# One group of the second block's modulation, moved from the heads' stage into an earlier norm

## The chip, the cores and the metric

The kernel runs on one core of one Trainium2 chip. The metric is the time of an execution on the device in microseconds (us); several executions were timed and their median counts.

## What is computed

Two transformer blocks in a row, 512 tokens of width 1024, all in float32. The first block: a mixer (RWKV and differential attention), a mixture of experts, and a token embedding that is gated and added. The second block has two layers, each with a mixer and a mixture of experts. Its norms and branches are modulated by vectors that depend on a condition `c` alone, not on the tokens:

```python
# first block, the end
ple_gate = jax.nn.sigmoid(rms_norm(x, norm_ple[l]) @ w_ple_gate[l])
x = x + ple_gate * (p[l] @ w_ple_proj[l])
# second block, for each layer l
mod = jax.nn.silu(c) @ ada_w[l] + ada_b[l]
mod_c = jax.nn.silu(c_ctx) @ ada_w[l] + ada_b[l]
sh1, sc1, g1, sh2, sc2, g2 = jnp.split(mod[:, None, :], N_MOD, axis=-1)
csh1, csc1, cg1, csh2, csc2, cg2 = jnp.split(mod_c, N_MOD, axis=-1)
h = modulate(rmsnorm(x, norm_mix_g[l]), sh1, sc1)     # h * (1 + scale) + shift
```

`ada_w` is 2 x 1024 x 6144. So the modulation is two rows times a matrix of 24 MB for each layer: almost all of it is the reading of the matrix.

## The kernel before

The program is a row of phases. Each is a block with its own semaphores, and a barrier of all engines closes it: the next phase starts when the latest engine of this one is done. A wait for that barrier shows in the trace as released by line 139. A scope that ends adds its semaphores to a list; when the list holds over 95 they are cleared, with one more barrier (line 144).

The modulation (`Modulation`, `ModulationSide`, line 2365 on) is cut into 2 x 3 groups `(l, g)`: layer `l`, 2048 of the 6144 columns. A group is carried as side work by some phase, and its result goes to the tensor `modD` in HBM, from which later norms load their scales and shifts as rows. The groups stand as follows: (0, 0) in `h1`, the heads' stage of the first block; (0, 1) in the differential attention `a1`; (0, 2) in the norm `ne` of the second block's first mixer; (1, 0) and (1, 1) in its heads' stage `he`; (1, 2) in the norm `no` of its second mixer. The groups of layer 1 are first read by `no`.

For one group the carrying phase does this:

- SyncE (`begin`, `sync`): 4 small loads of the bias, then 8 loads of 1 MB (128 partitions x 2048 columns, line 2420) into a ring of 3 buffers. From the fourth on a load is issued only when the matmuls of the piece three before it are done. At the end, 4 stores to `modD` (line 2413), and a wait for them.
- TensorE (`tensor`, lines 2451 and 2455): for each piece 4 matmuls with a moving operand of 512 columns and a stationary operand of 2 columns (each appears as two in the trace), and after the eighth piece 4 with the bias. The pieces are dealt out evenly over the phase's steps: with `total` pieces, step `s` of `steps` gets those from `total * s // steps` up to `total * (s + 1) // steps`.
- ScalarE (`scalar`, line 2435): 4 copies of 2 x 512 from PSUM, after all its other work in the phase.

`norm_phase` (line 201): ScalarE sums the squares of all tiles, a small chain gives the inverse root, VectorE scales tile by tile (line 303; with modulation also line 307), TensorE turns each tile with 8 transposes (line 324), ScalarE and VectorE write the high and the low half of the result (lines 179 and 184). The side work stands on TensorE behind the transposes of each tile. On SyncE it stands behind the loads of the gain and of `ahead`. `np` has 4 tiles, `ne` and `no` 6.

`ple` (line 2746) runs `np`, then `pq` (transposes of the embedding), then `lg` (the two matmuls, with their weights read in pieces of 256 KB). Its `early` loads the embedding, waits for it, and loads three pieces for `lg`, all on SyncE's queue during `np`.

`heads_phase` (line 504) in `he`: 12 jobs, in this order: four tiles of queries, four of keys (half as wide), then two of context queries and two of context keys. For each job VectorE scales and turns by the rotary tables (lines 597 to 610), TensorE transposes, ScalarE and VectorE split (lines 630 and 184). A second piece of side work, the pooling branch `PoolSide` (lines 2529, 2539, 2555, 2559, 2567), lies between. TensorE's order in a step is:

```python
for j, (i, t) in enumerate(jobs):
    if mix:
        mix.tensor(pe, j)
    if extra:
        extra.tensor(pe, j, len(jobs))
    pe.wait_ge(y_done, j + 1)
```

so that the transpose of job `j` stands behind the pieces of step `j`. After `he` comes the attention `ae`.

Of the kernel before, what the change touches and what calls it, by code (L numbers as in the profile page):

```python
# [194 lines left out]
def bc_row(ap, n):  # L195

    return ap.rearrange("(a n) -> a n", a=1).to_broadcast([P, n])
# [257 lines left out]
def linear(lhs, nk, tiles, W, cols, evac, on="v", behind=None):  # L455

    return dict(lhs=lhs, nk=nk, tiles=tiles, W=W, cols=cols, evac=evac, on=on, behind=behind)


def transpose_phase(nc, name, src, nt, nk, dst, tab, ahead=None):  # L460

    G = min(nk, 4)
    groups = [(t, k) for t in range(nt) for k in range(0, nk, G)]
    with Scope(nc, name) as s:
        banks = [s.ps(f"pt{i}") for i in range(4)]
        t_done, hi_done, lo_done = s.sem("t"), s.sem("hi"), s.sem("lo")
        block = s.block()

        def parts(i):
            t, k = groups[i]  # L470
            hi, lo = (d[:, k:k + G, t * P:(t + 1) * P] for d in dst)
            return hi, lo, banks[i % 4][:, 0:G * P].rearrange("p (k t) -> p k t", k=G)

        if ahead:
            @block.sync
            def _(sp):
                ahead.fetch(sp)

        @block.tensor
        def _(pe):  # L480
            for i, (t, k) in enumerate(groups):
                if i >= 4:
                    pe.wait_ge(lo_done, i - 3)
                for j in range(G):
                    mm = pe.transpose(banks[i % 4][:, j * P:(j + 1) * P], src(t, k + j), tab[:, C_IDENT:C_IDENT + P])
                mm.then_inc(t_done, 1)

        @block.scalar
        def _(act):
            for i in range(len(groups)):  # L490
                hi, _, bank = parts(i)
                act.wait_ge(t_done, i + 1)
                split_hi(act, hi, bank).then_inc(hi_done, 1)

        @block.vector
        def _(v):
            for i in range(len(groups)):
                hi, lo, bank = parts(i)
                v.wait_ge(hi_done, i + 1)
                split_lo(v, lo, bank, hi).then_inc(lo_done, 1)  # L500
# [2149 lines left out]
def operand(pair):  # L2650

    return lambda k, t: [h[:, k, t * P:(t + 1) * P] for h in pair]
# [90 lines left out]
            linear_phase(nc, "l5", [linear(operand(hT), KD, allt, A["w_out"], D, add_evac(xs))], ahead=ahead)  # L2743


def ple(nc, tab, A, xs):
    allt = lambda c: range(NT)
    with Scope(nc, "pl") as m:
        hT = m.pair("hT", [P, KD, SEQ])
        g = m.sb("g", [P, NT, D])  # L2750
        pt = m.sb("p", [P, NT, 256])
        pT = m.pair("pT", [P, 2, SEQ])
        p_in = m.sem("p")
        ahead = Ahead(m, "lg", A["w_ple_gate"], D, 3)

        def early(sp):
            sp.dma_start(pt[:, :, :], A["p"].rearrange("(t p) d -> p t d", p=P)).then_inc(p_in, 16)
            sp.wait_ge(p_in, 16)
            ahead.fetch(sp)
        norm_phase(nc, "np", xs, tab, A["norm_ple"], hT=hT, ahead=early)  # L2760
        transpose_phase(nc, "pq", lambda t, k: pt[:, t, k * P:(k + 1) * P], NT, 2, pT, tab)

        def gate_evac(act, link, ps, t, c):
            return act.activation(g[:, t, c * 512:(c + 1) * 512], ps, ACT.Sigmoid)

        def add(v, link, ps, t, c):
            gg = g[:, t, c * 512:(c + 1) * 512]
            link(v.tensor_tensor(gg, ps, gg, ALU.mult))
            x = xs[t][:, c * 512:(c + 1) * 512]
            return v.tensor_tensor(x, x, gg, ALU.add)  # L2770
        linear_phase(nc, "lg", [linear(operand(hT), KD, allt, A["w_ple_gate"], D, gate_evac, on="a"),
                                linear(operand(pT), 2, allt, A["w_ple_proj"], D, add, behind=0)], ahead=ahead)


def gated_add(rows_of, xs, G):

    def evac(v, link, ps, t, c):
        cs = slice(c * 512, (c + 1) * 512)
        link(v.tensor_tensor(ps, ps, G[rows_of(t)][:, cs], ALU.mult))
        return v.tensor_tensor(xs[t][:, cs], xs[t][:, cs], ps, ALU.add)  # L2780
    return evac
# [23 lines left out]
def even_mixer(nc, tab, A, xs, mod, modulation):  # L2805

    is_x = lambda t: 0 if t >= XT0 else 1
    with Scope(nc, "e1") as m:
        pj = m.sb("pj", [P, NTA, 1280])
        with Scope(nc, "e3") as r:  # L2810
            hT = r.pair("hT", [P, KD, NTA * P])
            mods = [(mod(j, 1), mod(j, 0)) for j in range(2)]
            ahead = Ahead(r, "le", A["even_w_in_2"], 1280, 3)
            norm_phase(nc, "ne", xs, tab, A["norm_mix_g_2"][0], hT=hT, mods=[mods[is_x(t)] for t in range(NTA)],
                       ahead=ahead.fetch, side=lambda s: modulation.side(s, [(0, 2)], 3))

            def evac(v, link, ps, t, c):
                n = min(512, 1280 - 512 * c)
                return v.tensor_copy(pj[:, t, c * 512:c * 512 + n], ps)
            linear_phase(nc, "le", [linear(operand(hT), KD, lambda c: range(NTA), A["even_w_in_2"], 1280, evac)], ahead=ahead)  # L2820
        oT = m.pair("oT", [P, 8, NTA * P])
        with Scope(nc, "e2") as q:
            qT, kT = q.pair("qT", [P, 4, NTA * P]), q.pair("kT", [P, 2, NTA * P])
            with Scope(nc, "e4") as w:
                pooled = [dict(nt=NT, u=lambda t: pj[:, XT0 + t, 768:1280], dst=[h[:, 4:8, XT0 * P:] for h in oT]),
                          dict(nt=XT0, u=lambda t: pj[:, t, 768:1280], dst=[h[:, 4:8, 0:XT0 * P] for h in oT])]
                keys = lambda t: pj[:, t, 512:640].rearrange("p (h d) -> p h d", d=64).unsqueeze(2).to_broadcast([P, 2, 2, 64])
                part = lambda t: pj[:, t, 0:512].rearrange("p (h e d) -> p h e d", e=2, d=64)
                turned = lambda d: (lambda t: tuple(h[:, :, t * P:(t + 1) * P] for h in d))
                rope = A["rope"][1]  # L2830
                rx, rc = range(XT0, NTA), range(XT0)
                common = dict(axes=2)
                heads_phase(nc, "he", tab, [
                    dict(src=part, heads=8, tiles=rx, gain=A["a_q_gain_2"], rope=lambda t: t - XT0, rope_src=rope, scale=0.125,
                         dst=turned(qT), **common),
                    dict(src=keys, heads=4, tiles=rx, gain=A["a_k_gain_2"], rope=lambda t: t - XT0,
                         rope_src=None, scale=1.0, dst=turned(kT), **common),
                    dict(src=part, heads=8, tiles=rc, gain=A["a_q_gain_2"], rope=None, rope_src=None, scale=0.125,
                         dst=turned(qT), **common),
                    dict(src=keys, heads=4, tiles=rc, gain=A["a_k_gain_2"], rope=None, rope_src=None,  # L2840
                         scale=1.0, dst=turned(kT), **common)], NTA * P,
                    side=lambda s: modulation.side(s, [(1, 0), (1, 1)], 3),
                    pool=lambda s: PoolSide(s, [A["band_x"], A["band_c"]], A["pool_w_2"], A["pool_scale_2"], pooled))
            attend_phase(nc, "ae", tab, even_pairs(qT, kT, lambda k, kv: pj[:, k, 640 + HD * kv:704 + HD * kv], oT), nk=(NTA, NTA),
                         start=0, prob=[q.sb(f"prob{i}", [P, NTA * P])[:, :] for i in range(4)],
                         row=[pj[:, i, 0:256] for i in range(2)])
        G = [m.sb(f"G{j}", [P, D]) for j in range(2)]
        linear_phase(nc, "lf", [linear(operand(oT), 8, lambda c: range(NTA), A["even_w_out_2"], D, gated_add(is_x, xs, G))],
                     loads=[(G[j][:, :], bc_row(mod(j, 2), D)) for j in range(2)])
# [84 lines left out]
def fused_blocks(nc, A, out, upto=None):  # L2934
# [8 lines left out]
    with nc.allow_non_contiguous_dma("parameter vectors, once"), Scope(nc, "g") as g:  # L2943
        tab = g.sb("tab", [P, C_END])
        x = g.sb("x", [P, NT, D])
        modulation = Modulation(g, tab, A["c_2"], A["c_ctx_2"], A["ada_w_2"], A["ada_b_2"], modD)
        xq = [x[:, t, :] for t in range(NT)]

        def stage(n):
            return upto is None or n in upto  # L2950
# [18 lines left out]
            moe(nc, "f1", tab, xq, A["norm_ffn"], None, None, A["w_group"], A["b_group"], A["w_expert_router"],  # L2969
                A["b_expert_router"], A["w_gate"], A["w_up"], A["w_down"], hbuf, ybuf)  # L2970
        if stage("ple"):
            ple(nc, tab, A, xq)
        ctx = g.sb("ctx", [P, XT0, D])
        xs = [ctx[:, t, :] for t in range(XT0)] + xq
        load_phase(nc, "lc", [(ctx[:, :, :], A["ctx_2"].rearrange("(t p) d -> p t d", p=P))])
# [79 lines left out]
```

## Time and profile before

| | us |
|---|---|
| median of three runs | 3744.28 |
| lowest, highest | 3737.8, 3747.65 |
| the profiled execution | 3746.24 |
| its span in the trace | 3744.4 |
| TensorE busy | 3152.3 (84%) |
| VectorE busy | 2458.5 (66%) |
| ScalarE busy | 1923.5 (51%) |

Times in the rows are microseconds from the start of the span. PE is TensorE, PEld its loads of the stationary operand, DVE VectorE, ACT ScalarE, POOL GpSimd, SP SyncE; a q behind an engine's name means its queue. Merged lines of a timeline give the start of the first, the time from there to the end of the last, and in brackets how long the engine had stood idle and what released it. The granted clock (PEclk) is a share of 2.4 GHz: 0.50 is 1.2 GHz.

### The profile page before, as it was taken

To read this page: it belongs to the slowest core of one execution; us is meant where nothing else is said; L and a number is where in the kernel's file an instruction comes from. 1 tells how busy PE (TensorE), PEld (TensorE's weight loads), DVE (VectorE), ACT (ScalarE), POOL (GpSimd) and SP (SyncE) were. 2 spreads that over 40 slices of the span, in tenths; PEclk is the share of its full clock that TensorE was granted. 3 is DMA by queue.
4 is the path that set the end of the run, shared out by engine and by line. 5 is a ranking of instruction groups with operands and counts; after the bars stand their busy time and mean duration, and the time that the engine had idled before them with its cause. 6 is when DMAs were issued, how large, how long until landed. Compare 5 with 4: busy or idle time off the path is not lost. (4 is left out here: it accounts for less than half of the span.)

```text
span 3744.4 us, 49560 instructions
## 1 busy us (share of the span) xinstructions
PE 3152.3 (84%) x18564; PEld 2577.7 (69%) x18564; DVE 2458.5 (66%) x2652; ACT 1923.5 (51%) x2169; POOL 562.6 (15%) x431
## 2 busy tenths in 40 slices
PE   7786957889999947959769999983998859999993
PEld 5685825668888835727568888871776648888883
DVE  3535255479999954255369999975215459999984
ACT  3312333267777733126137777753216537777762
POOL 0220000022222210001002222211004202222210
PEclk9898978789999978979869999996998969999997
DMA  4006641479999934250249999966111149999992
GB/s 125 1 4 225 207 172 58 143 265 368 374 374 368 366 130 158 69 205 7 89 182 374 376 377 384 371 250 242 45 46 29 58 162 377 373 365 364 361 349 104
DMA packets 227089, 832.62 MB, mean 222 GB/s; under 512 B 69734, under 2 KB 94182, under 8 KB 146300
## 3 DMA queue, kind: packets, MB, share of 16 engines
q1 hardware_dynamic: 195116, 786.16, 56.9%
q0 software_dynamic: 31680, 43.92, 3.4%
q8 instruction: 98, 1.61, 0.2%
q14 instruction: 51, 0.42, 0.0%
q10 hardware_dynamic: 144, 0.52, 0.0%
HBM read 816.53 MB, written 85.43 MB: 241 GB/s over the span
## 5 line engine op out<-in xcount | busy, mean ns | idle before, releaser
L184 DVE TENSOR_TENSOR f3e_w_lo<-f_raw,f3e_w_hi 128x2048 fp32r<-128x2048 f32 x198 | 446.4, 2285 | 5.1 <-ACT f3e_w_hi L179 5.1
L184 DVE TENSOR_TENSOR f1e_w_lo<-f_raw,f1e_w_hi 128x2048 fp32r<-128x2048 f32 x192 | 433.0, 2285 | 6.1 <-ACT f1e_w_hi L179 6.1
L184 DVE TENSOR_TENSOR f2e_w_lo<-f_raw,f2e_w_hi 128x2048 fp32r<-128x2048 f32 x192 | 433.5, 2285 | 5.4 <-ACT f2e_w_hi L179 5.3
L179 ACT ACTIVATE f3e_w_hi<-f_raw 128x2048 fp32r<-128x2048 f32 x198 | 370.9, 1910 | 0.2 <-issue 0.2
L179 ACT ACTIVATE f1e_w_hi<-f_raw 128x2048 fp32r<-128x2048 f32 x192 | 359.9, 1910 | 0.0
L179 ACT ACTIVATE f2e_w_hi<-f_raw 128x2048 fp32r<-128x2048 f32 x192 | 359.7, 1909 | 0.0
L190 PE MATMUL l_psum_acc<-l_w_hi,m_hT_hi 128*128 128x512 f32 x288 | 115.2, 400 | 33.2 <-DVE l_w_lo L184 33.2
L184 DVE TENSOR_TENSOR l_w_lo<-l_raw,l_w_hi 128x512 fp32r<-128x512 f32 x70 | 48.3, 692 | 122.5 <-ACT l_w_hi L179 122.3
L2023 POOL DMA_INDIRECT ybuf<-f1e_y,f_dst x32 | 69.7, 2179 | 342.3 <-DVE f1e_y L2229 331.8
L2023 POOL DMA_INDIRECT ybuf<-f2e_y,f_dst x32 | 67.8, 2119 | 341.1 <-DVE f2e_y L2229 341.1
L2023 POOL DMA_INDIRECT ybuf<-f3e_y,f_dst x32 | 67.8, 2119 | 340.5 <-DVE f3e_y L2229 340.5
L179 ACT ACTIVATE l_w_hi<-l_raw 128x512 fp32r<-128x512 f32 x70 | 44.2, 632 | 141.3 <-PE l_psum_acc L192 89.4
L191 PE MATMUL l_psum_acc<-l_w_lo,m_hT_hi 128*128 128x512 f32 x288 | 114.8, 399 | 0.0
L192 PE MATMUL l_psum_acc<-l_w_hi,m_hT_lo 128*128 128x512 f32 x288 | 114.8, 398 | 0.0
L190 PE MATMUL f3e_psum_gate<-f3e_w_hi,f3e_xT_hi 128*128 128x512 f32 x264 | 110.0, 417 | 3.3 <-DVE f3e_xT_lo L184 3.3
L190 PE MATMUL f3e_psum_y<-f3e_w_hi,f3e_hT_hi 128*128 128x512 f32 x264 | 104.1, 394 | 3.7 <-DVE f3e_hT_lo L184 3.7
L190 PE MATMUL f1e_psum_gate<-f1e_w_hi,f1e_xT_hi 128*128 128x512 f32 x256 | 106.5, 416 | 0.0
L190 PE MATMUL f2e_psum_gate<-f2e_w_hi,f2e_xT_hi 128*128 128x512 f32 x256 | 105.8, 413 | 0.0
L190 PE MATMUL f3e_psum_up<-f3e_w_hi,f3e_xT_hi 128*128 128x512 f32 x264 | 103.5, 392 | 2.1 <-DVE f3e_w_lo L184 2.1
L192 PE MATMUL f3e_psum_gate<-f3e_w_hi,f3e_xT_lo 128*128 128x512 f32 x264 | 104.3, 395 | 0.0
L191 PE MATMUL f3e_psum_gate<-f3e_w_lo,f3e_xT_hi 128*128 128x512 f32 x264 | 104.1, 394 | 0.0
L191 PE MATMUL f3e_psum_y<-f3e_w_lo,f3e_hT_hi 128*128 128x512 f32 x264 | 103.9, 394 | 0.0
(797 smaller groups left out, 8895.4 us busy)
## 6 DMA issues: line engine op xcount, KB each, us to landing
f_raw<-in_moe_w_dram SPq DMA_DIRECT2D x390, 1024.0 KB, 7.5
f_raw<-in_w_gate_dram SPq DMA_DIRECT2D x64, 1024.0 KB, 7.8
f_raw<-in_w_up_dram SPq DMA_DIRECT2D x64, 1024.0 KB, 7.3
f_raw<-in_w_down_dram SPq DMA_DIRECT2D x64, 1024.0 KB, 6.8
ybuf<-m_zeros SPq DMA_DIRECT2D x11, 2048.0 KB
he_adaw<-in_ada_w_dram SPq DMA_DIRECT2D x16, 1024.0 KB, 7.1
l_raw<-in_w_in_dram SPq DMA_DIRECT2D x56, 256.0 KB, 8.9
h_adaw<-in_ada_w_dram SPq DMA_DIRECT2D x8, 1024.0 KB, 6.2
```

What stands on the lines that cost most here:

```text
L179: return act.activation(dst, src, ACT.Copy)
L184: return v.tensor_tensor(dst, src, hi.bitcast(F32), ALU.subtract)
L190: pe.matmul(out, lh, rh, start=first, stop=False)
L191: pe.matmul(out, lh, rl, start=False, stop=False)
L192: return pe.matmul(out, ll, rh, start=False, stop=last)
L2023: pool.indirect_dma_start(out=ybuf, out_offset=bass.IndirectOffsetOnAxis(ap=R.dst[:, k - 1:k], axis=0), in_=y[:, :], in_offset=None, bound ...
```

## The change

Group (1, 0) leaves the heads' stage `he` and is carried by the norm `np`, as its side work with a ring of 3 of its own. `he` keeps group (1, 1). `ple` is handed the `modulation` object. The computation is the same.

```diff
-def ple(nc, tab, A, xs):
+def ple(nc, tab, A, xs, modulation):
...
-        norm_phase(nc, "np", xs, tab, A["norm_ple"], hT=hT, ahead=early)
+        norm_phase(nc, "np", xs, tab, A["norm_ple"], hT=hT, ahead=early, side=lambda s: modulation.side(s, [(1, 0)], 3))
...
-                    side=lambda s: modulation.side(s, [(1, 0), (1, 1)], 3),
+                    side=lambda s: modulation.side(s, [(1, 1)], 3),
...
         if stage("ple"):
-            ple(nc, tab, A, xq)
+            ple(nc, tab, A, xq, modulation)
```

## Rows read from the trace of the kernel before

**Rows 1.** The page, part 4: the chain that ended last, by engine.
```profile
ACT 0%; DVE 0%; DVEq 0%; issue 0%; ACTq 0%
```
**Rows 2.** Busy us of each engine by stretch, then granted clock, DMA share, GB/s.
```profile
1379.00:1400.00 21.00, 8.32 (x40) 7.08 (x40) 11.55 (x17) 12.33 (x23) 0.00 (x0) 0.58 0.27 88
...
1480.00:1485.00 5.00, 1.34 (x7) 1.34 (x8) 4.86 (x6) 0.19 (x1) 0.00 (x0) 0.50 1.02 426
...
1644.00:1676.00 32.00, 16.46 (x96) 3.92 (x88) 10.55 (x25) 9.01 (x18) 0.00 (x0) 0.74 0.52 198
```
**Rows 3.** Timeline of `np`: start, length, engine, line, operation, idle before.
```profile
1384.39 1.29 SPq L343 DMA_DIRECT2D pl_lgfirst<-in_w_ple_gate_dram  x3
...
1387.10 3.32 PE L324 MATMUL np_psum_pt<-g_tab,np_h 128*128 128x128 f32 x16 [38.88 <-DVE np_h L303]
...
1396.70 0.69 DVE L184 TENSOR_TENSOR pl_hT_lo<-np_psum_pt,pl_hT_hi 128x512 fp32r<-128x512 f32 x1 [0.16 <-ACT pl_hT_hi L179]
...
1397.71 1.94 PE L485 MATMUL pq_psum_pt<-g_tab,pl_p 128*128 128x128 f32 x8 [1.68 <-PEq L139]
```
**Rows 4.** Who waited for whom, 1592 to 1682: us in total, times, longest.
```profile
PE he_psum_ada L2451 <- DMA he_adaw<-in_ada_w_dram: 10.8, 8, 2.6
```
**Rows 5.** Timeline of `he`: transposes, pieces, row copies, and the first work of `ae`.
```profile
1634.96 0.44 PE L646 MATMUL he_psum_pt<-g_tab,he_work 128*128 128x128 f32 x2
...
1636.96 1.04 PE L2451 MATMUL he_psum_ada<-he_adaw,g_silu_c 128*2 128x512 f32 x8
...
1663.63 1.89 PE L2451 MATMUL he_psum_ada<-he_adaw,g_silu_c 128*2 128x512 f32 x8 [2.60 <-DMA he_adaw<-in_ada_w_dram]
...
1667.26 0.69 PE L646 MATMUL he_psum_pt<-g_tab,he_work 128*128 128x128 f32 x2
...
1668.27 4.87 ACT L2435 ACTIVATE he_adab<-he_psum_ada 2x512 f32<-2x512 f32 x8
...
1676.73 1.28 ACT L953 ACT_TABLE_LOAD   x1 [3.60 <-PEq L144]
```
**Rows 6.** Timeline of `ne`, which carries one group, and of the next block's first load.
```profile
1472.44 1.31 SPq L2402 DMA_DIRECT2D ne_adab<-in_ada_b_dram  x4
...
1473.79 23.15 SPq L2420 DMA_DIRECT2D ne_adaw<-in_ada_w_dram  x8
...
1485.56 1.89 PE L2451 MATMUL ne_psum_ada<-ne_adaw,g_silu_c 128*2 128x512 f32 x8
...
1493.03 1.04 PE L2451 MATMUL ne_psum_ada<-ne_adaw,g_silu_c 128*2 128x512 f32 x8 [0.87 <-DMA ne_adaw<-in_ada_w_dram]
...
1503.83 1.04 PE L2451 MATMUL ne_psum_ada<-ne_adaw,g_silu_c 128*2 128x512 f32 x8 [1.05 <-DMA ne_adaw<-in_ada_w_dram]
...
1505.91 2.43 ACT L2435 ACTIVATE ne_adab<-ne_psum_ada 2x512 f32<-2x512 f32 x4 [3.41 <-PE ne_psum_ada L2455]
...
1510.87 1.29 SPq L389 DMA_DIRECT2D le_raw<-in_even_w_in_dram  x3
```
**Rows 7.** Landing times of the weight loads (`h_adaw`) in stage `h1`.
```profile
DMA to landing us min/median/max: 4.8/6.2/8.8
```
**Rows 8.** Timeline of TensorE in `no`: the fourth and the eighth piece.
```profile
2587.93 1.04 PE L2451 MATMUL no_psum_ada<-no_adaw,g_silu_c 128*2 128x512 f32 x8 [0.15 <-DMA no_adaw<-in_ada_w_dram]
...
2598.81 1.04 PE L2451 MATMUL no_psum_ada<-no_adaw,g_silu_c 128*2 128x512 f32 x8 [0.21 <-DMA no_adaw<-in_ada_w_dram]
```
**Rows 9.** Timeline of VectorE in `he`: first instruction of jobs 4, 6, 8 and 9.
```profile
1632.65 0.41 DVE L597 TENSOR_TENSOR he_normed<-e_pj,he_stat 128x256 f32<-128x256 f32 x1
...
1638.22 0.41 DVE L597 TENSOR_TENSOR he_normed<-e_pj,he_stat 128x256 f32<-128x256 f32 x1
...
1646.87 0.68 DVE L597 TENSOR_TENSOR he_normed<-e_pj,he_stat 128x512 f32<-128x512 f32 x1
1649.23 0.68 DVE L597 TENSOR_TENSOR he_normed<-e_pj,he_stat 128x512 f32<-128x512 f32 x1
```
**Rows 10.** Timeline of TensorE in stage `h1`: a step's transpose.
```profile
518.55 0.66 PE L646 MATMUL h_psum_pt<-g_tab,h_work 128*128 128x128 f32 x4 [1.10 <-DVE h_work L610]
```

## Prediction

> **What bounds the kernel now.** I read the chain of waits first and put it away: its shares are all 0%, because it stops at the last stage's barrier [rows 1]. The kernel is a row of blocks, each closed by a barrier of all engines, so a block costs what its latest engine costs and the stages add up. The change touches two blocks, far apart: the norm `np` of the token embedding's stage and the heads' stage `he`. I therefore read the busy time by stretch for the two [rows 2], then the timeline of each, and the blocks that already carry one group of the modulation as models: `ne`, `no` and `h1`.
>
> `np` runs from 1379.0 to 1397.7 us and is bound by VectorE and ScalarE after a serial start. TensorE is busy 8.3 of 21 us, and the DMA engines 27% [rows 2]: that is the room that the group is moved into. The last low half is written by VectorE at 1396.70 + 0.69, and the next block's first matmul starts at 1397.71 [rows 3]. SyncE has long been done by then.
>
> `he` has two ends. Until about 1640 us VectorE sets the pace. From then on TensorE's instructions stand in line behind the pieces of the modulation, and these wait for their 1 MB transfers, in total 10.8 us in 8 waits [rows 4]. The last pieces go at 1663.63, the last transpose of heads stands behind them and starts at 1667.26, ScalarE copies the head out and then eight rows of the modulation (4.87 us), and the next block begins at 1676.73 [rows 5]. From 1644 to 1676 VectorE would fit in a third of the time (10.55 of 32 us) [rows 2].
>
> **What is added to `np`.** SyncE: 4 bias loads, 8 loads of 1 MB, 4 stores. TensorE: 8 pieces and the bias matmuls. ScalarE: 4 row copies. And the block's end now waits for the stores.
> - SyncE ends the three early loads of `lg` at 1384.39 + 1.29 = 1385.68 [rows 3]. In `ne` the bias loads begin at 1472.44 and the first weight load goes at 1473.79, 1.35 us later [rows 6]. So the first weight load goes at about 1387.05.
> - The first lands after 4.8 us, the least that stage `h1` shows [rows 7]: 1391.85. TensorE, whose transposes of two tiles take 3.3 us from 1387.10 [rows 3], is done with the first tile by then and waits. A piece at the low clock takes 1.89 us [rows 6]: done at 1393.7.
> - The ring has three buffers, so the fourth load is issued only then. In `ne` the first piece ends at 1485.56 + 1.89 = 1487.45 and the fourth starts at 1493.03, 5.6 us later [rows 6]: here 1399.3.
> - From the fourth piece to the eighth `ne` takes 1503.83 - 1493.03 = 10.8 us [rows 6], `no` 2598.81 - 2587.93 = 10.9 us [rows 8]. That is 2.7 us a piece, the stream of transfers at work: here 1410.15. The transposes of tiles 1 to 3 lie between the pieces (TensorE's order is tile, two pieces, tile), delayed, but they need under 2 us each and end before the last piece. Their evacuations on ScalarE and VectorE do too, so VectorE's old end at 1397.4 becomes slack.
> - From the start of the last piece to the next block `ne` takes 1510.87 - 1503.83 = 7.04 us: bias matmuls, four row copies from 1505.91 for 2.43 us, stores and barrier [rows 6]. Here the next block starts at 1417.2 instead of 1397.7: **+19.5 us**.
>
> Ends of this term: below, a stream at the rate of the stretch at 1480 us (426 GB/s [rows 2], 2.46 us a MB) without a pause: 1391.85 + 7 x 2.46 = 1409.1, so +18.4. Above, the whole of `ne`, 1503.83 - 1473.79 = 30.0 us from first issue to last piece [rows 6]: +26.4. I take 19.5, since `ne` had 2.5 MB of gains, scales and shifts and the early loads ahead of its first weight load, where `np` has only the early loads in flight.
>
> The trace's 426 GB/s is above what the Trainium skill names as the limit of transfers from HBM for one core, about 358 GB/s ("DMA: Bandwidth & Descriptors", section "Where 436 GB/s comes from"). By that figure, an estimate, a megabyte would take 2.93 us and the last piece would come 0.9 us later than by the rows.
>
> **What is taken from `he`.** SyncE: 4 bias loads, 8 weight loads, 4 stores. TensorE: half of 16 pieces and of the bias matmuls. ScalarE: 4 of 8 row copies. The 8 pieces left are spread over 12 steps (none in steps 0, 3, 6 and 9), and the loads are issued far ahead of use: the fourth follows the first piece, at step 1, and is wanted at step 5. So I expect no wait for a weight in this block, and VectorE sets the pace.
> - Steps 0 to 4 stay nearly as they are, the transpose of step 4 at 1634.96 [rows 5]. Removed pieces only open gaps here.
> - On VectorE jobs 4 and 5 take 1638.22 - 1632.65 = 5.57 us [rows 9]. Jobs 6 and 7 are of the same shape: job 8 starts at 1643.8. A context query job takes 1649.23 - 1646.87 = 2.36 us [rows 9], two of them: 1648.5. Job 10 has half the width and no pool piece, estimated from these rows at 1.5 us, job 11 at 0.9: heads ready at 1650.9.
> - TensorE gives job 10's transpose at about 1649.6, then the last piece and the bias matmuls, each some 1.0 us at the high clock (1.04 in [rows 5]): the last transpose starts at about 1652.0, not at 1667.26.
> - From there to the next block it was 1676.73 - 1667.26 = 9.47 us [rows 5]. Four row copies of eight are gone, half of 4.87: 7.04. The next block starts at 1659.0: **-17.7 us**.
>
> Ends: at most, VectorE alone decides and the last transpose is at 1650.9: -18.8. At least, only TensorE's waits for weights go (10.8 us [rows 4]) and four row copies (2.4): -13.2. I take 17.7, as the pieces themselves leave TensorE's line too.
>
> **Nothing else** moves. `np` gets nine more semaphores. Counted from the code, the clearing of semaphores (past 95) still falls behind `he`, with 110 instead of 101, and nowhere new. The next block `pq` starts after the same kind of pause.
>
> **Sum:** +19.5 - 17.7 = +1.8 us. The profiled execution has a span of 3744.4 us and took 3746.24 us; it would become 3746.2 and 3748.0. The median of the runs shown is 3744.28, 2.0 below that execution, so 3746.1 us for the median. The gain in `he` is paid back in `np`, because a group costs about the same where it is the stage's last work: eight transfers, a ring of three, and a serial tail.
>
> **Rivals.**
> - A, `he` gives back less (-13.2, the lower end above): +6.3 us. For it: VectorE and ScalarE wait for each other through the pool pieces. Against: VectorE is idle most of the stretch. 3750.6 us.
> - B, the ring in `np` is as slow as in `ne` (+26.4): +8.7, 3753.0 us. For it: TensorE's order puts two pieces before the next tile, so a late piece also delays the release of a buffer. Against: the heavy loads ahead of `ne`'s first are missing.
> - C, slower for good: TensorE's clock. With half of its pieces gone TensorE pauses in `he`, and the granted clock, a mean of 0.74 from 1644 to 1676 [rows 2], may fall to 1.2 GHz from step 4 on. A piece then takes 1.89 instead of 1.04 us [rows 5], six such items +5.1 us. The transpose, band and pool matmuls of a step, 2.0 us from 1634.96 to 1636.96 [rows 5], would double as well, in four steps up to +8, of which some 3 lie in TensorE's slack: about +10 in all, net +12, 3756 us. It decides as soon as a step of TensorE is over VectorE's 2.8 us. Against it: in `h1` TensorE pauses 1.10 us in each step and its transposes keep the short form of 0.66 us [rows 10]. The Trainium skill ("TensorE: Matmul & The Clock Gate", section "Part 1: The HAM clock gate (the "warmup" mystery)") says that the throttled clock is the default and activity releases it; it speaks for this rival.
> - D, faster: both terms at their kind ends, +18.4 and -18.8: -0.4. No row gives more than that, so a gain past 0.3% would come from outside the two blocks. 3744 us.
>
> **How the numbers follow.** Forecast 0.6 (3746.1), A 0.15, B 0.1, C 0.08, D and anything outside 0.07. About 0.3%, 11 us, is what a measurement can tell from no change. The forecast, A, B and D lie within it, C just past it. The three runs spread over 10 us, so some of each spills. Faster 0.05, same 0.86, slower 0.09. The range takes in D less that scatter and B plus some of it: 3738 to 3756.
>
> **What the profile would show.** `pq`'s first matmul near 1417; TensorE waiting for DMA in `np` in nearly every piece from the third on; the row copies there from about 1412. The start of `ae` only some 2 us behind 1676.73 [rows 5], though `he` itself starts 19.5 later; no wait for `he_adaw` after its first piece, and VectorE without gaps over 1 us after step 5. Wrong if `np` grows by over 22 us (the ring), or `he` shrinks by under 15 (waits other than for weights, or the clock), or if any other stage changes by over 1 us.

## The result: 5.6 us more, within 0.3%

| | us |
|---|---|
| median of 20 executions, before | 3741.07 (3732.8 to 3747.65) |
| median of 20 executions, changed | 3746.18 (3738.46 to 3754.72) |
| ratio, 95% interval | 1.0015 [1.0008, 1.0022]: +5.6 us, +3.0 to +8.2 |
| profiled execution of the changed kernel | 3741.43, span 3739.6 |

The changed kernel is slower, by an amount that no single execution shows and 20 of each do. The forecast was +1.8 us and 3746.1; the time lies in the range and the sign was right. That the time agrees to 0.1 us is luck: the forecast started from a median of 3744.28 over three runs, 3.2 above the 3741.07 over 20, and had the difference 3.8 too small.

The profiled execution, 3741.43 us, is a quick one: it is faster than the profiled one of before (3746.24), though the medians stand the other way. So a comparison of the two spans would give the wrong sign. I read lengths of blocks instead, each from its own start: `np` from its first square to the first matmul of `pq`, `he` from its first load to the first matmul of `ae`.

The changed `np`, timeline:

```profile
1376.38 1.06 ACT L261 ACTIVATE np_sq<-g_x 128x1024 f32<-128x1024 f32 x1 [3.57 <-PEq L139]
...
1382.30 1.28 SPq L343 DMA_DIRECT2D pl_lgfirst<-in_w_ple_gate_dram  x3
1383.63 1.20 SPq L2402 DMA_DIRECT2D np_adab<-in_ada_b_dram  x4
1384.87 18.28 SPq L2420 DMA_DIRECT2D np_adaw<-in_ada_w_dram  x8
...
1391.27 1.89 PE L2451 MATMUL np_psum_ada<-np_adaw,g_silu_c 128*2 128x512 f32 x8 [4.83 <-DMA np_adaw<-in_ada_w_dram]
...
1399.23 1.04 PE L2451 MATMUL np_psum_ada<-np_adaw,g_silu_c 128*2 128x512 f32 x8 [1.19 <-DMA np_adaw<-in_ada_w_dram]
...
1409.58 1.04 PE L2451 MATMUL np_psum_ada<-np_adaw,g_silu_c 128*2 128x512 f32 x8 [1.40 <-DMA np_adaw<-in_ada_w_dram]
...
1411.65 2.42 ACT L2435 ACTIVATE np_adab<-np_psum_ada 2x512 f32<-2x512 f32 x4 [4.42 <-PE np_psum_ada L2455]
1414.10 1.14 SPq L2413 DMA_DIRECT2D modD<-np_adab  x4
```

Against [rows 3], where `pq` began 18.7 us after the start of `np`, it begins here at 1416.65, 40.3 us after it. In between stands what the prediction named: the loads behind the early ones, a wait before nearly every piece, then row copies and stores one after the other. TensorE's waits in `np`, with the total, the times and the longest:

```profile
PE np_psum_ada L2451 <- DMA np_adaw<-in_ada_w_dram: 10.6, 7, 4.8
```

The changed `he`, which answers to [rows 4, 5]. There is no wait for `he_adaw` any more:

```profile
1617.90 0.33 SPq L539 DMA_DIRECT2D he_gain<-in_a_q_gain_dram  x1
...
1642.77 1.04 PE L2451 MATMUL he_psum_ada<-he_adaw,g_silu_c 128*2 128x512 f32 x8
...
1653.27 0.44 PE L646 MATMUL he_psum_pt<-g_tab,he_work 128*128 128x128 f32 x2
...
1668.21 1.04 PE L2451 MATMUL he_psum_ada<-he_adaw,g_silu_c 128*2 128x512 f32 x8
...
1670.15 0.44 PE L646 MATMUL he_psum_pt<-g_tab,he_work 128*128 128x128 f32 x2
...
1670.90 2.41 ACT L2435 ACTIVATE he_adab<-he_psum_ada 2x512 f32<-2x512 f32 x4
...
1677.01 1.28 ACT L953 ACT_TABLE_LOAD   x1 [3.71 <-PEq L144]
```

Busy time by stretch for the two blocks, columns as in [rows 2]: the DMA engines' share in `np` has gone from 0.27 to 0.70, and TensorE's granted clock over `he` is 0.79, and 1.00 in its first piece.

```profile
1376.40:1416.60 40.20, 16.51 (x104) 5.69 (x104) 10.47 (x14) 13.10 (x23) 0.00 (x0) 0.71 0.70 256
1617.90:1677.00 59.10, 29.31 (x172) 14.86 (x172) 42.81 (x119) 21.88 (x45) 0.00 (x0) 0.79 0.54 182
```

### The profile page after: what moved, and what is told of

The parts are those of the page before. It is cut to its first block and busy times, and to the rows that moved or that the text cites. A ratio compares the mean times of both kernels' runs of the same rounds, so it can differ in the third digit from the quotient of the medians.

```text
span 3739.6 us, 49562 instructions
## 1 busy us (share of the span) xinstructions
PE 3139.4 (84%) x18564; PEld 2568.8 (69%) x18564; DVE 2457.2 (66%) x2652; ACT 1922.8 (51%) x2169; POOL 561.9 (15%) x431
## 5 line engine op out<-in xcount | busy, mean ns | idle before, releaser
L192 PE MATMUL f3e_psum_up<-f3e_w_hi,f3e_xT_lo 128*128 128x512 f32 x264 | 102.9, 390 | 0.0
```

Of the source, the lines that this page charges most:

```text
L192: return pe.matmul(out, ll, rh, start=False, stop=last)
```

## The experiments

Lengths are in us, each from one trace of the kernel, blocks measured as above. "First piece" and "last" are the starts of TensorE's first piece in `np` and of the last matmul of the eighth, from the start of `np`. Runs without a ratio were timed once. A ratio with an interval is against before.

| run | ratio | `np` | first piece, last | `he` |
|---|---|---|---|---|
| before | | 18.7 | | 79.0 |
| before_b, before_c | | 18.7, 18.7 | | 75.2, 79.2 |
| changed | 1.0015 [1.0008, 1.0022] | 40.3 | 14.9, 33.6 | 59.2 |
| after_again | 1.0016 [1.0005, 1.0028] | 42.4 | 15.7, 35.8 | 59.1 |
| take_only | 0.9944 [0.9928, 0.996] | 18.7 | | 61.0 |
| add_only | 1.0047 [1.0031, 1.0063] | 41.2 | 14.8, 34.6 | 74.7 |
| he_8loads | | 18.7 | | 67.7 |
| np_3loads | | 34.0 | 14.4, 27.3 | 61.1 |
| np_ring8 | | 39.4 | 15.3, 32.7 | 59.3 |
| np_first3 | | 36.7 | 10.0, 30.1 | 59.2 |
| np_first8 | 1.0001 [0.999, 1.0012] | 33.1 | 10.0, 26.5 | 59.1 |
| early_w | 1.0019 [1.0008, 1.003] | 38.8 | | 60.6 |
| early_wg | 0.9979 [0.9969, 0.9989] | 30.8 | 3.0, 22.5 | 60.9 |

### The two halves

The theory: the stages add up, so each half alone shows its term. The rival: the measured sum comes from somewhere else. take_only drops group (1, 0) and computes it nowhere:

```diff
-                    side=lambda s: modulation.side(s, [(1, 0), (1, 1)], 3),
+                    side=lambda s: modulation.side(s, [(1, 1)], 3),
...
-            rows = [[modD[l, j, i * D:(i + 1) * D] for i in range(6)] for j in range(2)]
+            rows = [[modD[l if i > 1 else 0, j, i * D:(i + 1) * D] for i in range(6)] for j in range(2)]
```

> Half of the change: group (1, 0) is gone from the heads' stage and is computed nowhere. The second mixer's norm reads layer 0's rows in its place, so that its loads stay the same; that part of the result is another one. Theory (two independent blocks): the stage he, 79.0 us in the kernel before and 59.1 in the changed one from its first load to the first instruction of ae, is 59 to 61 here, and np stays at 18.7. Whole kernel 19 to 20 us below the kernel before. Rival (part of he's gain in the changed kernel was the chance moment at which TensorE's clock rose): he is 61 to 63 and the whole gain 16 to 18. Rival (only waits for weights go, my rival A): 65.8, gain 13.

add_only is the changed kernel with `[(1, 0), (1, 1)]` kept in `he`, so that the group is computed twice:

> The other half: group (1, 0) is computed in np and, as before, in he too; the result is the same. Theory: np, 18.7 us in the kernel before and 40.3 in the changed one from its first square to the first matmul of pq, is 40 to 41, he stays at 79, and the whole kernel is 20 to 23 us above the kernel before, the sum with the other half being +2 to +4. Rival (something outside the two blocks makes up the measured +5.6 against the +2.9 that the two traces show): the two halves together give +5 or more, and a third stage differs by over 1 us in this trace or the other.

Measured, by the ratios: -20.9 us and +17.6 us, each with some 6 us either way (the medians are 3720.52, 3740.56 and 3758.96, differences of -20.0 and +18.4). By the blocks, taking the group out leaves `he` at 61.0, where the first piece takes 1.89 us; that is the length that the expectation gave to its rival, the moment at which TensorE's clock rises. Adding it makes `np` 41.2, and `he` came out at 74.7, not at the 79 expected. Each half has its sign and about its size. Their sum, -3.3, is no reading: the two intervals together are wider than what is looked for. TensorE at the end of `he`, first take_only, then add_only:

```profile
1624.03 1.89 PE L2451 MATMUL he_psum_ada<-he_adaw,g_silu_c 128*2 128x512 f32 x8
...
1652.38 0.44 PE L646 MATMUL he_psum_pt<-g_tab,he_work 128*128 128x128 f32 x2
1659.21 0.80 PE L876 MATMUL ae_psum_score<-e_kT_hi,e_qT_hi 64*128 64x512 f32 x2 [6.39 <-PEq L144]
```

```profile
1684.75 1.04 PE L2451 MATMUL he_psum_ada<-he_adaw,g_silu_c 128*2 128x512 f32 x8 [1.78 <-DMA he_adaw<-in_ada_w_dram]
...
1686.68 0.54 PE L646 MATMUL he_psum_pt<-g_tab,he_work 128*128 128x128 f32 x2
1696.09 0.80 PE L876 MATMUL ae_psum_score<-e_kT_hi,e_qT_hi 64*128 64x512 f32 x2 [8.87 <-PEq L144]
```

With both groups the last piece waits for its transfer and the pause to `ae` is 8.87 us; with one group there is no such wait and the pause is 6.39. In take_only `he` starts at 1598.16, so the last transpose is 54.2 us in and `ae` 61.0.

### How much one trace says

before_b and before_c are the kernel before, unchanged; after_again is the changed one, unchanged. The question was whether 79.0 in the first trace of `he` and 40.3 in the first of `np` are typical.

> The kernel before once more, for its trace. Unchanged blocks of the study's traces vary: he with both groups took 79.1 us (first load to the first matmul of ae) in the first trace and 74.7 in the half that only adds, where its instructions are the same ones. Theory (the first trace was a long one, so the +2.9 us read from two single traces is too small, and the typical sum is near the +6 measured over many runs): he lies between 74 and 78 here. Rival (79 is typical, and the surplus over +2.9 comes from elsewhere): 78.5 or more.

> The same again, a second draw: theory 74 to 78 us for he, rival 78.5 or more. np stays at 18.7 in both, by either.

> The changed kernel itself, beside its two halves on one chip. Theory: +2 to +4 us against the kernel before, np at 40 to 41 and he at 59 to 61. Rival (+5.6 is the real size): +5 to +8, with the surplus in he (a later rise of TensorE's clock) or outside both blocks.

`he` with both groups is 79.03, 75.21, 79.20 and 74.71 (add_only) long: mean 77.04. So 79 is not an exception, and before_c came out as its rival, but it is the upper end. after_again missed too: `np` is 42.4 where 40 to 41 was expected, and the ratio is about +6 us where the theory said +2 to +4. The last piece in before_b:

```profile
1658.28 1.04 PE L2451 MATMUL he_psum_ada<-he_adaw,g_silu_c 128*2 128x512 f32 x8 [1.42 <-DMA he_adaw<-in_ada_w_dram]
1659.25 1.04 PE L2455 MATMUL he_psum_ada<-he_adab,g_tab 1*2 1x512 f32 x8
1660.22 0.44 PE L646 MATMUL he_psum_pt<-g_tab,he_work 128*128 128x128 f32 x2
```

It takes 1.04 us here and 1.89 in [rows 5]. There TensorE had waited 1.66 and 2.60 us before its last two pieces, and the granted clock from the last one on is 0.50 (1.2 GHz); here it had waited 1.09 and 1.42 us, and the clock is 1.00. That is 0.85 us each for the piece and the bias matmuls behind it, 1.7 of the 3.8 us between the two executions. Of the rest 1.9 us lie before the last piece: it starts 65.9 us into the block in the first trace and 64.0 here, while 39.2 us in the two are level.

`np` with the group as in the change is 40.3, 42.4 and 41.2: mean 41.3. `he` with one group, in the nine kernels of the table that have it so, is 59.15, 59.12, 61.05, 61.06, 59.35, 59.22, 59.09, 60.64 and 60.88: mean 59.95. So the blocks give +22.6 - 17.1 = **+5.5 us**, and 20 executions gave +5.6. Agreement this close is partly luck: four values of `he` that spread over 4.5 us fix their mean to little better than an us (an estimate). The two profiled executions alone give +21.6 - 19.9, and 1.2 us between `pq` and `he`: +2.9.

Part of the spread goes with one thing, the moment at which the clock rises in `he`: the piece at 1642.77 of the changed kernel, 24.9 us into its `he`, took 1.04 us, that at 1624.03 of take_only, 25.9 us into its own, still 1.89 (both lines are shown above; the granted clock is 1.00 and 0.50). Where the clock is up by 25 us the transpose of step 4 comes 35.3 to 35.7 us in, where it rises later 36.8 to 37.3, with one group or with two. Among the kernels with one group the early ones are 59.1 to 59.4 long and the late ones 60.6 to 61.1. It may be more than chance, though this was seen only afterwards: it is early in all six traces of kernels that load all eight pieces within `np` (changed, after_again, add_only, np_ring8, np_first3, np_first8) and late in the eight others, before's three among them. What ties the two blocks, 200 us apart, no run shows.

### What `he` gives back

he_8loads is the kernel before with both groups in `he`, but only the first eight megabytes loaded; the other pieces reuse what is in the buffers:

```diff
+        self.loads = 8 if groups == [(1, 0), (1, 1)] else 16
...
-            if n >= self.ring:
+            if n < self.loads and n >= self.ring:
...
-            sp.dma_start(self.W[n % self.ring][:, :], src).then_inc(self.w_in[n % self.ring], 16)
+            if n < self.loads:
+                sp.dma_start(self.W[n % self.ring][:, :], src).then_inc(self.w_in[n % self.ring], 16)
...
-            pe.wait_ge(self.w_in[n % self.ring], 16 * (n // self.ring + 1))
+            if n < self.loads:
+                pe.wait_ge(self.w_in[n % self.ring], 16 * (n // self.ring + 1))
```

> The kernel before, with all 16 pieces of he on TensorE and its 8 row copies, but only the first 8 loads: the pieces of group (1, 1) multiply what lies in the ring and wait for nothing, so that group's result is another one. It splits he's gain (79.0 to 59.1 us). Rival A (the waits for weights are the gain): 79.0 - 10.8 = 68 or more remains only if the pieces themselves cost little, and then the step to 59 is row copies and steps where TensorE is late. Theory (waits carry most of it; a piece more in a step costs 1.0 us only where TensorE is later than VectorE): he is 62 to 66, of which 2.4 are row copies.

TensorE at the end of its `he`, which starts at 1594.4:

```profile
1649.98 1.90 PE L2454 MATMUL he_psum_ada<-he_adaw,g_silu_c 128*2 128x512 f32 x16
...
1652.78 0.44 PE L646 MATMUL he_psum_pt<-g_tab,he_work 128*128 128x128 f32 x2
1662.03 0.79 PE L876 MATMUL ae_psum_score<-e_kT_hi,e_qT_hi 64*128 64x512 f32 x2 [8.81 <-PEq L144]
```

`he` is 67.7 long, so I had sized it too short. The clock rises late here, so it is to be compared with the traces in which it does so too: 77.8 is the mean of before's three, 60.9 that of the four with one group. From 77.8 to 67.7 the loads are worth some 10 us; from 67.7 to 60.9 eight pieces, the bias matmuls and four row copies are worth 6.7. Of these the row copies are 2.4: the pause to `ae` is still 8.81, against 6.39 in take_only. Some 4 us are left for the pieces and bias matmuls in TensorE's line (two pieces, 1.90 us, still stand right before the last transpose), less what remains of waits: one of 1.23 us for the eighth load falls into this part. The stretch itself says the same: from the transpose of step 4 to the last it is 21.1 us here and 16.9 in take_only. It is one trace, and executions of one kernel differ by some 4 us in this block; but rival A, 13.2 for the whole, let only the waits and the copies go, and the means say 17.1.

### What makes `np` long

np_3loads loads three of the eight megabytes. np_ring8 has a buffer for each piece. Both are the changed kernel otherwise.

> The changed kernel with only 3 of the 8 loads in np; the later pieces multiply what lies in the ring and wait for nothing, so group (1, 0) comes out different. All matmuls, copies and stores are as in the changed kernel. Theory (np is bound by its transfers): 5 loads fewer take away 5 x 2.5 us at most, the rest is the tiles' own work behind the second piece, which now sets the end: np 30 to 32 us instead of 40.3. Rival (TensorE's work and its order set the end): np above 36.

> The changed kernel with 8 buffers in np's ring, the order of the loads left as it is. Theory (transfers follow each other at 2.45 us a MB, and the ring of 3 costs only small gaps, 18.3 us from first to eighth piece against 7 x 2.45 = 17.2): np 39 to 40 us. Rival (the ring of 3 is the bound): under 37.

With three loads `np` is still 34.0: the five others cost some 7 us of 41.3, and the tail, TensorE's order and the first landing make the rest. It fell between theory and rival: the stream of transfers ends last in `np`, but TensorE's own line would end only some 7 us earlier. The ring of three costs at most 1.9 us (39.4 against 41.3), within what two executions differ by: rival B's mechanism is small.

np_first3 and np_first8 put the loads ahead of the embedding's and `lg`'s, with rings of 3 and 8:

```diff
+            if first:
+                extra.begin(sp)
+                extra.load(sp)
```

> The changed kernel with the group's loads in np moved ahead of the embedding's load, its wait and the early loads, the ring left at 3. It tells the order from the ring, and whether the first load lands 4.8 us after its issue (as in h1) when nothing but the gain is in front of it, where it took 6.4 in the changed kernel. Theory: first load issued about 2 us after the first square instead of 8.5 and landed by 8, np 35 to 37 us. Rival (the late landing has nothing to do with the early loads): over 6 us from issue to landing here too.

> The changed kernel with one thing more: in np the group's loads go ahead of the embedding's load, its wait and the three early loads, behind the gain alone, and its ring has 8 buffers, so that no load waits for TensorE. Theory (np is bound by 8 MB of transfers in a row and a serial tail of 7 us): the loads start some 7 us earlier and run at 2.45 us a MB; the last piece starts about 24 us after the first square, np is 31 to 33 instead of 40.3, and the kernel is 5 to 8 us below the kernel before. Rival (TensorE's order, two pieces before each tile, is what holds np): np stays above 37.

The first weight load goes 1.9 us after the start in both instead of 8.5. The issues of SyncE in np_first8:

```profile
1380.90 0.33 SPq L247 DMA_DIRECT2D np_gain<-in_norm_ple_dram  x1
1381.27 1.53 SPq L2407 DMA_DIRECT2D np_adab<-in_ada_b_dram  x4
1382.84 5.28 SPq L2429 DMA_DIRECT2D np_adaw<-in_ada_w_dram  x8
...
1408.31 1.28 SPq L348 DMA_DIRECT2D pl_lgfirst<-in_w_ple_gate_dram  x3
1411.49 1.15 SPq L2420 DMA_DIRECT2D modD<-np_adab  x4
```

The eight loads are issued in 5.28 us, yet the last lands 19.3 us after its issue: from there on the transfers alone set the pace, a megabyte each 2.5 us, and the block is 33.1 long. From the blocks it would be +14.4 - 17.1 = -2.7 us against before, and 1.0001 [0.999, 1.0012], -3.7 to +4.5 us, agrees; my expectation for the kernel, 5 to 8 us below before, was too hopeful.

np_first3 also bears on the first landing. Here is the time from the issue of the first weight load to its landing, changed kernel, then np_first3, where nothing but the gain and the bias is ahead of it (the others: 5.9 in np_3loads, 6.2 in add_only, 7.1 in after_again, 7.2 in np_ring8, 6.8 in np_first8):

```profile
np_adaw<-in_ada_w_dram SPq DMA_DIRECT2D x1, 1024.0 KB, 6.3
```

```profile
np_adaw<-in_ada_w_dram SPq DMA_DIRECT2D x1, 1024.0 KB, 6.1
```

So the early loads are not what makes the first one late: some 6 to 7 us is what it takes here, and the 4.8 of [rows 7] was the least of eight. The loads behind it move beside it: in np_first3 the DMA engines moved some 2.1 MB in these 6 us (242, 377 and 430 GB/s in three stretches of 2 us), twice the load that landed.

### Loads from a gap before `np`

The stretch before `np` has room: from 1350 to 1360 us in the trace of before almost nothing moves (share of the DMA engines in the last but one column), before `f1c` starts to gather its rows at 1360.15. The two versions below do not use that gap itself: they issue later, when the gathers of the third tile have landed, some 6 to 8 us before `np` begins.

```profile
1350.00:1355.00 5.00, 0.00 (x0) 0.00 (x0) 0.06 (x1) 0.00 (x0) 0.78 (x1) 0.74 0.05 16
1355.00:1360.00 5.00, 0.00 (x0) 0.00 (x0) 0.00 (x0) 0.00 (x0) 0.00 (x0) 0.50 0.00 0
1360.00:1379.00 19.00, 0.00 (x0) 0.00 (x0) 10.04 (x8) 4.59 (x4) 7.93 (x8) 0.50 0.64 221
```

early_w issues six of the eight loads at the end of `f1c`, into stream buffers that are free by then, and puts TensorE's pieces before each tile's transposes:

```diff
+            if ready:
+                sp.wait_ge(y_in[2][1], 16)
+                ready.fetch(sp)
...
+        self.deal = [0, 4, 6, 8, 8] if ready else None
```

> A version meant to beat both: group (1, 0) is still carried by np, but six of its eight loads are issued by SyncE in the block before (the experts' combine f1c, into the experts' own six weight buffers, free by then), once the gathers of the third tile have landed; the other two have buffers of their own. TensorE takes four pieces before the first tile's transposes, two before the second, two and the bias before the third. Theory (np in the changed kernel is bound by 8 MB in a row behind a late first issue, and a serial tail of 7 us that stays): np 24 to 28 us instead of 40 to 42, f1c longer by under 2, he as in the changed kernel, the whole 8 to 13 us below the kernel before. Rival (the transfers slow the last gathers and the gain's load, which stands behind them): np over 30 or f1c longer by over 3, and no more than 4 us below the kernel before.

The rival held: by the ratio the kernel is some 7 us slower than before. The norm's gain is loaded after them on the same queue; SyncE and VectorE in early_w:

```profile
1374.11 4.12 SPq L2396 DMA_DIRECT2D f_raw<-in_ada_w_dram  x6
1382.03 0.33 SPq L247 DMA_DIRECT2D np_gain<-in_norm_ple_dram  x1
...
1395.69 0.18 DVE L288 RECIPROCAL np_ss<-np_ss 128x4 f32<-128x4 f32 x1 [8.51 <-DMA np_gain<-in_norm_ple_dram]
```

```profile
np_gain<-in_norm_ple_dram SPq DMA_DIRECT2D x1, 512.0 KB, 13.6
```

Half a megabyte behind six landed 13.6 us after its issue, against 3.9 in before, and every tile of `np` waited for it (the sixth of the six had landed at about 1394.4, the gain at 1395.6). early_wg also loads the gain first, ahead of the six, and issues the last two weight loads at once when `np` begins:

```diff
+        sp.dma_start(self.G[:, :], bc_row(self.gain, D)).then_inc(self.g_in, 16)
         for k in range(self.n):
...
+        self.deal = [0, 3, 5, 7, 8] if ready else None
```

> As the version before it (loads of the group started in the combine f1c), with what held that one taken away: in early_w the gain's load stood behind six megabytes in SyncE's queue and landed 13 us after its issue, and the norm waited for it. Here the gain is loaded in f1c ahead of the six weight loads, the two last weight loads go at once in np, ahead of the embedding's load and the early loads, and TensorE takes three pieces before the first tile's transposes, two before the second and third, one and the bias before the fourth. Theory (it was only the order of the queue): np 25 to 29 us (38.8 in early_w, 40 to 42 in the changed kernel), f1c as in early_w some 2 us longer than before, he 59 to 61, the whole 5 to 10 us below the kernel before. Rival (the transfers are simply late, 8 MB beside the gathers take until 1405): np over 33 and no gain that can be measured.

```profile
1370.81 0.33 SPq L2404 DMA_DIRECT2D f_readygain<-in_norm_ple_dram  x1
1371.19 4.33 SPq L2407 DMA_DIRECT2D f_raw<-in_ada_w_dram  x6
...
1380.52 1.89 PE L2495 MATMUL np_psum_ada<-f_raw,g_silu_c 128*2 128x512 f32 x8 [34.32 <-DMA f_raw<-in_ada_w_dram]
...
1390.48 1.04 PE L2495 MATMUL np_psum_ada<-f_raw,g_silu_c 128*2 128x512 f32 x8 [1.42 <-DMA f_raw<-in_ada_w_dram]
...
1399.22 1.53 PE L2495 MATMUL np_psum_ada<-np_adaw,g_silu_c 128*2 128x512 f32 x8
```

Its first piece stands 3.0 us after the start of `np` (1377.54) instead of 14.9, `np` is 30.8 long, 10.5 less than in the change, and the ratio is 0.9979 [0.9969, 0.9989]: 7.9 us faster than before by the ratio, -11.6 to -4.1, which is also below the changed kernel. It missed the length expected by some 2 us. The price in `f1c` is small: 19.4 us from the first gathered row to `np`, against 18.9. The blocks of its one trace give only +12.1 - 17.1 + 0.5 = -4.5 us; that lies just inside the interval, and where the rest comes from, if it is real, was not followed. The step from early_w changes three things at once (the gain first, the last two weight loads early, the order of the pieces), so how much of it is the queue's order alone is not shown.

## Why the prediction was right, by its steps

**Right.** The sign and the mechanism (the time, to 0.1 us, by luck, as said above): `np` is bound by the stream of eight transfers and a serial tail, and `he` gives back somewhat less than that costs. The steps that held, with the changed kernel's profiled execution: from the fourth to the eighth piece 1409.58 - 1399.23 = 10.35 (10.8 foreseen); from the last piece to `pq` 7.07 (7.04); in `he` from the transpose of step 4 to the last 1670.15 - 1653.27 = 16.9 (17.04); from there to `ae` about 6.9 (7.04); the last transpose behind the last piece and the bias matmuls, as foreseen, and no wait for a weight. VectorE runs in that stretch without a pause over 0.2 us until its last tile. One reading was off: of the 10.8 us of waits that I put behind 1640 us, 1.68 belong to the first piece, at 1614.95 ([rows 4] counts the whole block).

**Mis-sized: the first landing in `np`.** I took "the least that stage `h1` shows", 4.8 us; it was 5.9 to 7.2 in the seven traces named above. The median of the same row, 6.2, would have been within this. The issue was 0.4 us later than I had it, since the embedding, for which SyncE waits, landed later. So the first piece stood at 14.9, 15.7 and 14.8 us (changed, after_again, add_only) instead of 12.8: +2.3 on the mean. The pieces that follow took 18.7, 20.1 and 19.7 us instead of 18.7, another +0.8. That is the 3.1 us between +19.5 and +22.6. The value lay inside my bounds for the term (+18.4 to +26.4), and past the 22 us that I had called wrong. But the ring, to which I gave that case, is worth under 2 us of it.

**Right by offset: the gain of `he`.** "Steps 0 to 4 stay nearly as they are" holds at equal clock: the transpose of step 4 comes 37.2 us in before and 37.3 in take_only. In the changed kernel it comes at 35.4, because the clock is up earlier there; the working had no term for that. From one profiled execution to the other the gain is then 1.9 for this, 15.4 from step 4 to the last transpose (15.3 foreseen) and 2.6 behind it (2.4 foreseen): 19.9. On the means it is 17.1, since before's profiled `he` was a long one, 79.0 against 77.0, and the nine with one group are on the mean 0.8 us longer than the changed one's 59.15. The forecast of 17.7 lay between: a long execution to start from and the missing term pull opposite ways.

**The rivals.** A did not happen: `he` gave back 17.1, and by he_8loads some 3 to 4 of it are the pieces themselves. B's mechanism, the ring, is worth under 2 us by np_ring8 (one trace), against the 6.9 that B adds to the forecast. A's sum, +6.3, is the nearest to the measured +5.6 all the same: it has the right size for a wrong reason, since it took from `he` what was missing in `np`. C did not happen: in all nine traces with one group the matmuls of the pieces take 591 to 594 ns each from 30 us into `he` to its end, which is the clock of the piece of 1.04 us. So the Trainium skill's rule that I quoted for it ("TensorE: Matmul & The Clock Gate", section "Part 1: The HAM clock gate (the "warmup" mystery)"), that the throttled clock is the default and activity releases it, did not tell here: TensorE pauses in this block, for up to 1.57 us in the changed kernel's second half, but the clock had risen by 30 us in and the pieces stayed short in all nine.

**"If any other stage changes by over 1 us."** Some do between the two profiled executions, `f1e` by 2.7 us, with the same instructions: its last stretch of matmuls starts at 1339.80 in before and 1339.85 in the changed kernel, and takes 0.63 us a matmul for 5 us there and 0.39 here, the two levels of the clock. Its scatter is not known, since only these two traces were compared. The means over the two blocks account for +5.5 of +5.6; with their uncertainty an us or two could still lie elsewhere.

The Trainium skill's other rule that I had weighed, some 358 GB/s as the limit of transfers from HBM for a core ("DMA: Bandwidth & Descriptors", section "Where 436 GB/s comes from"), would make a megabyte 2.93 us, an estimate; the Trainium skill works the figure out there as half of what two cores share. In early_wg five pieces follow each other from 1380.52 to 1390.48 at 2.49 us, 421 GB/s: by this trace it is no limit where, as here, the program runs on one core, as [rows 2] already said.

## What to carry to other kernels

Side work that a stage carries is free only as far as the stage has slack behind its last piece: moved into a block that is shorter than its transfers, a group costs the whole stream, the landing of the first load and the serial tail. Start such transfers before the block, some 6 us before it in early_wg, and put the small load that everybody waits for ahead of the large ones in the queue (a start in the wholly idle stretch before that was not tried). For a difference of a few microseconds compare lengths of blocks in several executions of each kernel, and take the median of a row of landings, not the least.

## What was unexpected of the hardware

- Half a megabyte behind six on one queue landed 13.6 us after its issue, with little ahead 3.9: here the queue served the loads in the order of issue.
- The same block with the same instructions was 74.7 to 79.2 us long in four executions, partly by when TensorE's clock rose or fell; in fourteen traces the moment of the rise went with which kernel ran, though `np` ends 200 us before `he`. One profile of each kernel gave +2.9 us where 20 executions gave +5.6.
